# The last tile of the second feed-forward block, computed in two halves of 256 tokens, each with its own final norm, scaling and stores

## The reference

```python
def rmsnorm(x, g):
    x32 = x.astype(jnp.float32)
    y = x32 * lax.rsqrt(jnp.mean(x32 * x32, axis=-1, keepdims=True) + EPS)
    return y.astype(x.dtype) * g

def swiglu(h, w_in, w_out):                     # w_in 1024 x 5632, w_out 2816 x 1024
    gate, up = jnp.split(h @ w_in, 2, axis=-1)
    return (jax.nn.silu(gate) * up) @ w_out
...
    x = x + 0.5 * swiglu(rmsnorm(x, ffn2_norm[l]), ffn2_w_in[l], ffn2_w_out[l])
    return rmsnorm(x, final_norm)
```

## Time and profile before

| | us |
|---|---|
| median of 3 runs | 1888.96 (1887.38 to 1889.33) |
| the profiled execution, its own time | 1890.32 |
| its span | 1888.3 |
| PE busy | 1827.4 (97% of the span) |
| DVE busy | 1035.7 (55%) |
| ACT busy | 729.0 (39%) |
| from the last matmul's start (1872.40) to the end of the span | 15.9 |

### The profile page before, as it was taken

How to read it: one execution, slowest core, us unless ns; L and a number is a source line. 1 busy time by engine, 2 the same in 40 slices (tenths; PEclk the granted TensorE clock), 3 DMA queues, 4 the chain that set the end, 5 groups by cost and what they waited for, 6 DMA issues and landing times.

```text
span 1888.3 us, 20951 instructions
## 1 busy us (share of the span) xinstructions
PE 1827.4 (97%) x8276; PEld 1460.4 (77%) x8276; DVE 1035.7 (55%) x1484; ACT 729.0 (39%) x1197; POOL 53.8 (3%) x122
## 2 busy tenths in 40 slices
PE   6899999998999899999999999999999999999997
PEld 5677776877866578888888878888888888888886
DVE  6888876666477556444433336555443554444333
ACT  4577776333356643333222243222222333323221
POOL 2000101100120000000000000000000000000000
PEclk9999999999999999999999999999999999999998
DMA  4121212222211023333333422333333333332331
GB/s 149 66 68 67 79 56 78 92 89 70 90 59 34 12 89 91 106 94 100 95 93 94 132 78 80 99 101 92 98 101 100 90 96 94 101 98 90 103 93 53
DMA packets 47041, 163.82 MB, mean 87 GB/s; under 512 B 5216, under 2 KB 5472, under 8 KB 46944
## 3 DMA queue, kind: packets, MB, share of 16 engines
q1 hardware_dynamic: 46656, 162.29, 27.5%
q10 hardware_dynamic: 288, 0.20, 0.0%
HBM read 160.37 MB, written 2.10 MB: 86 GB/s over the span
## 4 chain that ended last, share of the span: by engine, by line
PE 86%; DVE 7%; ACT 4%; issue 2%; POOL 0%; DMA 0%; SPq 0%; DVEq 0%; ACTq 0%; POOLq 0%
PE pb L676 26%; PE pb L678 25%; PE pb L677 25%; PE pb L761 2%; PE pb L868 1%; DVE wl L1324 1%; PE pb L873 1%; PE pb L970 1%; PE pb L972 1%; PE pb L971 1%; DVE XL L1342 1%; ACT wr L1030 1%; PE pb L896 1%; PE pb L686 1%; DVE LL L1561 1%
## 5 line engine op out<-in xcount | busy, mean ns | idle before, releaser
L676 PE MATMUL pb<-XR,wr 128*128 128x512 f32 x1592 | 633.5, 398 | 24.0 <-DVE wl L1324 12.7
L677 PE MATMUL pb<-XL,wr 128*128 128x512 f32 x1592 | 623.5, 392 | 0.0
L678 PE MATMUL pb<-XR,wl 128*128 128x512 f32 x1592 | 623.1, 391 | 0.0
L1324 DVE TENSOR_TENSOR wl<-raw,wr 128x1024 fp32r<-128x1024 f32 (+1 forms) x298 | 359.5, 1206 | 409.9 <-ACT wr L1030 409.0
L1030 ACT ACTIVATE wr<-raw 128x1024 fp32r<-128x1024 f32 (+1 forms) x298 | 309.5, 1038 | 269.3 <-PE pb L678 243.4
L676 PEld LDWEIGHTS pb<-XR,wr 128*128 128x128 f32 x1592 | 301.5, 189 | 97.5 <-issue 27.0
L678 PEld LDWEIGHTS pb<-XR,wl 128*128 128x128 f32 x1592 | 301.0, 189 | 63.8
L677 PEld LDWEIGHTS pb<-XL,wr 128*128 128x128 f32 x1592 | 301.4, 189 | 60.2 <-issue 0.3
L1039 ACT ACTIVATE SQ<-H 128x512 f32<-128x512 f32 x42 | 26.4, 632 | 129.8 <-DVE H L1488 61.2
L676 PE MATMUL pb<-ffn1HR,wr 128*128 128x512 f32 x176 | 68.5, 389 | 0.0
L677 PE MATMUL pb<-ffn1HL,wr 128*128 128x512 f32 x176 | 68.5, 389 | 0.0
(11 more groups left out here) (315 smaller groups left out, 2229.0 us busy)
## 6 DMA issues: line engine op xcount, KB each, us to landing
raw<-in_ffn_in SPq DMA_DIRECT2D x88, 512.0 KB, 3.5
raw<-in_mix_in SPq DMA_DIRECT2D x48, 512.0 KB, 3.5
raw<-in_ssm_in SPq DMA_DIRECT2D x41, 512.0 KB, 3.3
raw<-in_ffn_out SPq DMA_DIRECT2D x32, 512.0 KB, 3.5
raw<-in_ffn_out SPq DMA_DIRECT2D x16, 384.0 KB, 3.1
raw<-in_mla_in SPq DMA_DIRECT2D x11, 512.0 KB, 3.2
raw<-in_ssm_out_a SPq DMA_DIRECT2D x8, 512.0 KB, 3.2
raw<-in_ssm_out_b SPq DMA_DIRECT2D x8, 512.0 KB, 3.3
```

Source lines behind the costliest of these rows:

```text
L676: e.matmul(o, r, xr, start=first, stop=False)
L677: e.matmul(o, r, xl, start=False, stop=False)
L678: return e.matmul(o, l, xr, start=False, stop=last)
L1324: e.tensor_tensor(wl[j % NS][:, 0:width(j)], raw[j % NR][:, 0:width(j)], wr[j % NS][:, 0:width(j)].bitcast(F32), ALU.subtract).then_inc(s_ ...
```

## The change

Tile 7 of the second feed-forward (`last_tile` on PE) is made in two passes over its 22 weight tiles, each with 256 tokens (p = 0: tokens 0 to 255, p = 1: 256 to 511) and each into a bank of its own. The three weight units of the tile are taken in the first pass and stay in their buffers for the second. The norm is made for each half: the sum over the partitions takes `ACC` (tiles 0 to 6) and `TB` (the square of tile 7, which ACT writes there) as two accumulating matmuls for each 128 tokens, in place of the fold of tile 7. The sums and the spread of half 0 are issued on PE inside the second pass, before weight tiles 7 and 17; DVE scales five tiles of half 0 before the residual of half 1 and three behind it. Stores are 128 x 256; SP issues all of half 0 and the even tiles of half 1, ACT the odd tiles of half 1.

```diff
@@ def place_ffn (banks)
-        for c in range(KT):
+        for c in range(KT if f == 0 else KT - 1):
             bk.place((name, 2, c), ring.next(), ...)
+        if f == 1:
+            for p in range(2):
+                bk.place(("last", p), ring.next(), (s_last, p + 1), (s_res, 40 + p))
+                b = 3 if p == 0 else ring.next()
+                bk.place(("sum", p), b, ...)
+                bk.place(("spread", p), b, ...)
@@ SP
-        for n in range(KT):
-            w.wait_ge(s_fin, n + 1)
-            e.dma_start(out[n], H[:, n, :]).then_inc(s_out, 16)
-        w.wait_ge(s_out, 16 * KT)
+        for p in range(2):
+            tk = slice(256 * p, 256 * p + 256)
+            for n in range(KT):
+                if p == 0 or n % 2 == 0:
+                    w.wait_ge(s_fin, 8 * p + n + 1)
+                    e.dma_start(out[n][:, tk], H[:, n, tk]).then_inc(s_out, 16)
+        w.wait_ge(s_out, 32 * KT)
@@ PE
+        def last_sums(p):
+            o = opened(("sum", p))
+            w.wait_ge(s_fold, sq.folded["fin", 6])
+            w.wait_ge(s_lastsq, p + 1)
+            for i in (2 * p, 2 * p + 1):
+                tk = slice(128 * i, 128 * i + 128)
+                e.matmul(o[:, i:i + 1], ACC[:, tk], ones[:, 0:1], start=True, stop=False)
+                m = e.matmul(o[:, i:i + 1], TB[:, tk], ones[:, 0:1], start=False, stop=True)
+            m.then_inc(s_sums, 1)
+        def last_spread(p):
+            o = opened(("spread", p))
+            w.wait_ge(*rooted[f"fin{p}"])
+            for i in (2 * p, 2 * p + 1):
+                m = e.transpose(o[:, 128 * i:128 * i + 128], RN[:, i:i + 1].to_broadcast([128, 128]), ident[:, :])
+            m.then_inc(s_spread, 1)
+        def last_tile():
+            parts = []
+            for p in range(2):
+                o = opened(("last", p))
+                tk = slice(256 * p, 256 * p + 256)
+                for t in range(FT):
+                    if p == 1 and t == 7:
+                        last_sums(0)
+                    if p == 1 and t == 17:
+                        last_spread(0)
+                    if p == 0 and t % 8 == 0:
+                        parts.append(take("ffn2_out", 21 + t // 8))
+                    r, l = parts[t // 8]
+                    w.wait_ge(s_hlo, FT + t + 1)
+                    s = slice(128 * (t % 8), 128 * (t % 8) + 128)
+                    m = three(o[:, tk], r[:, s], l[:, s], HRS[1][:, t, tk], HLS[1][:, t, tk], t == 0, t == FT - 1)
+                m.then_inc(s_last, 1)
+            last_sums(1)
+            last_spread(1)
@@ ACT
+        for p in range(2):
+            tk = slice(256 * p, 256 * p + 256)
+            w.wait_ge(s_res, 40 + p)
+            e.activation(TB[:, tk], H[:, 7, tk], ACT.Square).then_inc(s_lastsq, 1)
+        for n in range(1, KT, 2):
+            w.wait_ge(s_fin, 8 + n + 1)
+            e.dma_start(out[n][:, 256:512], H[:, n, 256:512]).then_inc(s_out, 16)
@@ DVE (newton takes the columns k; last_residual, last_root, last_scale are residual,
@@      root and scaling of the tokens or columns of half p)
-        fold("fin", 7)
-        root("fin")
-        w.wait_ge(*bk.full["spread fin"])
-        for n in range(KT):
-            e.scalar_tensor_tensor(out=H[:, n, :], ...).then_inc(s_fin, 1)
+        fold("fin", 6)
+        last_residual(0)
+        last_root(0)
+        last_scale(0, range(5))
+        last_residual(1)
+        last_scale(0, range(5, KT))
+        last_root(1)
+        last_scale(1, range(KT))
```

More of the change, by code:

```diff
@@ L437, in build_in @@
     s_e, s_es, s_proj, s_mg, s_mghi, s_mglo = [sem("s_" + n) for n in ("e", "es", "proj", "mg", "mghi", "mglo")]
-    s_fin = sem("s_fin")
+    s_last, s_lastsq, s_fin = sem("s_last"), sem("s_lastsq"), sem("s_fin")
     seq = unit_order()
@@ L446, in build_in @@
     spreads = {n: i for i, n in enumerate(("x", "g0", "g1", "g2", "g3", "kv", "ck", "cq", "both", "first", "mix", "f2",
-                                           "fin"))}
+                                           "fin0", "fin1"))}
     sums_no = {n: i + 1 for i, n in enumerate(("x", "g0", "g1", "g2", "g3", "kv", "ck", "cq", "m1", "m2", "mx", "f2",
-                                               "fin"))}
-    rooted = {n: (s_root, i + 1) for i, n in enumerate(("x", "kv", "first", "both", "mx", "f2", "fin"))}
+                                               "fin0", "fin1"))}
+    rooted = {n: (s_root, i + 1) for i, n in enumerate(("x", "kv", "first", "both", "mx", "f2", "fin0", "fin1"))}
     rooted.update({n: (s_groot, i + 1) for i, n in enumerate(("g0", "g1", "g2", "g3", "ck", "cq"))})
@@ L453, in build_in @@
     root_of = {"both": RQ, "ck": RT, **{n: GN for n in ("g0", "g1", "g2", "g3", "cq")}}
-    taken = {n: i + 1 for i, n in enumerate(("x", "g0", "g1", "g2", "g3", "kv", "ck", "cq", "m", "m2", "mx", "f2", "fin"))}
+    taken = {n: i + 1 for i, n in enumerate(("x", "g0", "g1", "g2", "g3", "kv", "ck", "cq", "m", "m2", "mx", "f2", "fin0",
+                                            "fin1"))}
     def whole(name, n):
@@ L462, in build_in @@
     sizes = {"x": 8, "g0": 4, "g1": 4, "g2": 4, "g3": 4, "kv": 8, "ck": 2, "cq": 3, "m1": 8, "m2": 8, "mx": 8, "f2": 8,
-             "fin": 8}
+             "fin": 7}
     accs = {n: TB if n in ("g1", "g3", "m2") else ACC for n in sizes}
@@ L588, in place_ffn @@
                 bk.place("spread f2", 3, (s_spread, spreads["f2"] + 1), (s_rs, 5))
-        for c in range(KT):
+        for c in range(KT if f == 0 else KT - 1):
             bk.place((name, 2, c), ring.next(), whole(name + "_out", 3 * c + 2), (s_res, 16 * (f + 1) + c + 1))
+        if f == 1:
+            for p in range(2):
+                bk.place(("last", p), ring.next(), (s_last, p + 1), (s_res, 40 + p))
+                b = 3 if p == 0 else ring.next()
+                bk.place(("sum", p), b, (s_sums, sums_no[f"fin{p}"]), (s_sv, taken[f"fin{p}"]))
+                bk.place(("spread", p), b, (s_spread, spreads[f"fin{p}"] + 1), (s_fin, 8 * p + 8))
     place_ffn(0)
@@ L617, in build_in @@
     place_ffn(1)
-    bk.place("sum fin", 3, (s_sums, sums_no["fin"]), (s_sv, taken["fin"]))
-    bk.place("spread fin", 3, (s_spread, spreads["fin"] + 1), (s_fin, 8))
     def ffn_turn(f, j):
@@ L1009, in _ @@
         ffn(1)
-        sums("fin")
-        spread("fin")
+        last_tile()
     @block.scalar
@@ L1241, in ffn @@
                     hi()
-                after_residual(2 * f + 2, c, ("mx", "fin")[f], 5, gain)
+                if f == 0 or c < KT - 1:
+                    after_residual(2 * f + 2, c, ("mx", "fin")[f], 5, gain)
         def second_mixer():
@@ L1346, in then, with newton @@
             return sem_ if last else c.up()
-        def newton(dst, done):
-            e.tensor_scalar(dst[:, :].bitcast(I32), SV[:, :].bitcast(I32), -0.5, float(0x5F3759DF), ALU.mult,
+        def newton(dst, done, k=slice(0, 4)):
+            e.tensor_scalar(dst[:, k].bitcast(I32), SV[:, k].bitcast(I32), -0.5, float(0x5F3759DF), ALU.mult,
                             ALU.add).then_inc(c.up(), 1)
@@ L1353, in newton @@
                 w.wait_ge(c.h, c.n)
-                e.scalar_tensor_tensor(out=SS[:, :], in0=dst[:, :], scalar=1.0, in1=dst[:, :], op0=ALU.mult,
+                e.scalar_tensor_tensor(out=SS[:, k], in0=dst[:, k], scalar=1.0, in1=dst[:, k], op0=ALU.mult,
                                        op1=ALU.mult).then_inc(c.up(), 1)
                 w.wait_ge(c.h, c.n)
-                e.scalar_tensor_tensor(out=SS[:, :], in0=SS[:, :], scalar=-0.5, in1=SV[:, :], op0=ALU.mult,
+                e.scalar_tensor_tensor(out=SS[:, k], in0=SS[:, k], scalar=-0.5, in1=SV[:, k], op0=ALU.mult,
                                        op1=ALU.mult).then_inc(c.up(), 1)
                 w.wait_ge(c.h, c.n)
-                m = e.scalar_tensor_tensor(out=dst[:, :], in0=SS[:, :], scalar=1.5, in1=dst[:, :], op0=ALU.add,
+                m = e.scalar_tensor_tensor(out=dst[:, k], in0=SS[:, k], scalar=1.5, in1=dst[:, k], op0=ALU.add,
                                            op1=ALU.mult)
@@ L1798, in ffn @@
                 w.wait_ge(s_hn, 8)
-                residual(2 * f + 2, n, (name, 2, n), half=True)
-                after_residual(n, ("mx", "fin")[f], 5, gain)
+                if f == 0 or n < KT - 1:
+                    residual(2 * f + 2, n, (name, 2, n), half=True)
+                    after_residual(n, ("mx", "fin")[f], 5, gain)
         def second_mixer():
@@ L1915, in _, with last_residual, last_root, last_scale @@
         ffn(1, None)
-        fold("fin", 7)
-        root("fin")
-        w.wait_ge(*bk.full["spread fin"])
-        for n in range(KT):
-            e.scalar_tensor_tensor(out=H[:, n, :], in0=H[:, n, :], scalar=col("final_norm", n), in1=PB[3][:, :],
-                                   op0=ALU.mult, op1=ALU.mult).then_inc(s_fin, 1)
+        fold("fin", 6)
+        def last_residual(p):
+            tk = slice(256 * p, 256 * p + 256)
+            w.wait_ge(*bk.full["last", p])
```

(16 more changed lines are left out.)

## The result

The changed kernel takes 1884.17 us (median of 19 runs, 1882.12 to 1888.60) against 1888.96 (19 runs, 1885.34 to 1891.30); the ratio is 0.9978, with a 95% interval of 0.9971 to 0.9985. In a second comparison, on another occasion, the same kernel gave 0.9988 (0.9979 to 0.9997). So it is faster, by 0.22% in the one and 0.12% in the other.

The account below looks back on a forecast made before the run. PE, busy 97% of the span, was taken to bound the kernel, with an exposed chain behind tile 7. Terms +2.12 (PE stream), +0.13 (late residual) and -4.57 (shorter chain) gave -2.3: 1888.96 to 1886.6 us, range 1884.5 to 1890.0.

Parts of the forecast that it names:

- 132 matmuls of 256: PE's tile 7 stream: 66 matmuls of 512 columns become 132 of 256 at pitch 0.120, costing +0.87 us.
- sums 0 in the stream: PE's second pass: half 0's partition sums, eight records, run inside the stream without waiting, costing +0.98 us.
- spread 0 in the stream: PE's second pass: half 0's two spread transposes run inside the stream without waiting, costing +0.27 us.
- residual 1 late behind DVE: DVE after the second pass: half 1's residual waits behind the fifth scaling of half 0, costing +0.13 us.
- residual, square, fold: Chain behind the stream: residual 0.27 less, square on ACT 0.21 less, fold gone for 0.70 less.
- sums 1 at the full clock: Half 1's sums on PE start sooner after the last matmul, at full clock: 0.95 us, 0.82 less.
- transposes: Half 1's spread on PE: two transposes instead of four, 0.43 us less if the clock has dropped by then.
- end of the stores: Last scaling to span end, 2.66 us: smaller store up to 0.3 sooner, ACT's issue 0.1 or 0.3 later; taken as 0.
- Rival B: PE's 256-wide pairs bound by weight loads or issue: pitch 0.137 to 0.17 (chance 0.11) or about 0.20 (0.04).
- A: Rival on PE's tile 7 stream: cheaper pitch, 0.108 to 0.113, total -3.3 to -4.0, time 1885.3; chance 0.25.
- C: Rival: half 0's spread or scalings on DVE come late, half 1's residual waits; -1.0 in all, 1887.9; chance 0.2.
- D: Rival: half 0's sums or spread stall PE in the second pass, up to 2.3 us; no chance of its own.

Follow-up runs that it names:

- e6: Kernel before with tile 7's matmuls in four passes of 128 tokens, norm, scaling and stores whole; time 1906.14 us.
- e4: Kernel before with whole-tile stores split, SP even and ACT odd tiles; 30.56 us from tile 7's start to the span's end (30.61 before).
- e1: Changed kernel with all stores of half 1 issued by SP, none by ACT; ratio to the kernel before 0.9987 (0.9978 to 0.9996).
- e8: Changed kernel with all eight stores of half 1 issued by ACT; 28.49 us from tile 7's start to the span's end (27.70 changed kernel).
- c1: Kernel before with two unused semaphores added; ratio to the kernel before 1.0004 (0.9995 to 1.0014).
- e3: Kernel before with only tile 7's matmuls in two passes of 256 tokens, norm, scaling and stores whole; ratio 1.0006 (0.9997 to 1.0014).
- e2: Changed kernel with four scalings of half 0 before the residual of half 1, not five; ratio to the kernel before 0.9985 (0.9977 to 0.9994).
- e5: Kernel before with 9 spare 512-wide matmuls ahead of sums and of spread; 29.41 us from tile 7's start to the span's end (30.61 before).

## Why the prediction was right, and where its sum was off

| step | forecast | measured |
|---|---|---|
| 132 matmuls of 256 | +0.87 | +0.86 (pitch 0.120) |
| sums 0 in the stream | +0.98 | +0.89 |
| spread 0 in the stream | +0.27 | +0.21 |
| residual 1 late behind DVE | +0.13 | +0.19 |
| residual, square, fold | -1.18 | -1.23 |
| sums 1 at the full clock | -0.82 | -0.74 |
| transposes | -0.43 | -0.43 |
| scaling | -2.14 | -2.13 |
| end of the stores | 0 | -0.52 |
| sum | -2.3 | -2.9 |

The measured column is the difference of the profiled executions; for instance sums 0 is 1864.89 - 1863.88, less one pitch of 0.12. Every step of the mechanism was there, in its place.

*The pitch* was taken from the same stream at 512 columns, streaming halved and the rest kept. That hit 0.120, but e6 shows that the reasoning was only half of it: at 256 the streaming is as long as the load, and one step further the load rules. Rival B was closer than the argument made it look: with four passes in place of two the stream costs 14 us more.

*The mis-sized term* is the stores: "Half the bytes might land up to 0.3 sooner, ACT's issue might be 0.1 or 0.3 later; I take 0." No row stood behind the 0.3 or behind ACT's delay. The last store landed 2.2 after its issue before and 1.7 with the change, 0.5 sooner, and ACT issued it 0.03 after the last scaling, no later than SP had; that is the 0.52 but for 0.02. With e4, where ACT issues the last whole tile and it lands after 2.2 as well, it is the smaller store and not the other queue that lands sooner. The step also said that both queues keep up because an issue takes 0.33 on SP. That duration is for 256 KB stores every 0.66 us; when a queue gets a store every 0.39 an issue takes 0.45 to 0.47 (e1, e8), and with one queue the gain would have turned into a loss of 0.2. It came out right because each queue had every second store.

*The clock term* rested on one transition of one execution. c1, e3, e4 and the kernel before have the same chain there, and their sums took 1.63, 1.02, 1.70 and 1.77: the drop fell 0.2 after their start in c1 and e4, behind them in e3, and 0.1 after their start before. With the change the sums ran 1.06 from their start to the root in all five profiles that share its order on PE (its own two, e1, e2 and e8), and e5 shows what the clock alone is worth, 1.20. But the margin was thin. The sums of half 1 run from 1.5 to 2.5 us behind the start of the last matmul. The clock dropped 4.3 behind it in the first profile, 2.4 in the second and in e1, upon the last of the eight records. In e6, whose PE stood idle behind its tile as before, it dropped after 1.9. So the 0.74 was likely, not certain.

*The rivals.* A (a cheaper stream) failed: 0.120, not 0.108 to 0.113. B failed at 256 in both its halves (0.120, against 0.137 and 0.20) and is real at 128. C and D failed: sums and spread had 1.4 to spare where 1.3 was forecast, and the residual was late by 0.19, which e2 takes back.

*The median* moved by 4.8 in the first comparison and 2.0 in the second (1887.43 to 1885.41), around the tail's 2.9. Of the 2.4 us between 1886.6 and 1884.17 the sum's error explains 0.6; the rest is scatter ahead of tile 7, for which the prediction had no term. The chance of 0.22 for over 0.2% faster fits two comparisons of which one came out over it.

## What to carry to other kernels

Splitting the last tile along tokens moves half of the epilogue beside matmuls, but it pays in the stream: here 2.0 us of PE work for 5.0 us of exposed chain, and only down to the width at which a matmul still covers its weight load. Put a price on the split from the pitch of the narrowest matmuls with full weight loads that the trace has. Halving a store also doubles the rate at which a queue must issue; check the issue against the pace of the producer, not against the old rows.

## What was not expected of the hardware

- An issue of a 128 x 256 store takes 0.33 to 0.35 us when the queue had 0.79 between stores, 0.45 to 0.47 when they are ready every 0.39 and follow back to back; 0.47 to 0.48 then pass from one to the next, on SP and ACT alike.
- The last store lands 2.2 us after its issue with 256 KB and 1.7 with 128 KB.
- Where PE had only the norm's small matmuls behind its last tile, the granted clock dropped 1.9 to 4.3 us after the last large matmul's start, in ten profiles.
- A fp32r matmul with its own 128 x 128 load has a pitch of 0.227, 0.120 and 0.112 us at 512, 256 and 128 columns, at the full clock.
- The same program's tile 7 started 4.1 us apart in two profiles (1853.45 and 1857.53), more than the whole change is worth.
